# Hybrid attention block: VectorE's read of query sums ahead of the tile rotation, GpSimd's power as a step behind it

## The reference

```python
h = rms_norm(x, norm_g)
z = h @ w_in
aq, ak, av, ag, mq, mk, mv, mi, mf, mo, mgate = jnp.split(z, split_points(), axis=-1)
q = rms_norm(aq.reshape(B, L, 16, 64), q_norm_g)
k = rms_norm(ak.reshape(B, L, 2, 64), k_norm_g)
q = apply_partial_rope(q, cos, sin)
k = apply_partial_rope(k, cos, sin)
ya = sliding_window_sink_attention(q, k, v, sink) * jax.nn.silu(ag)
...
x = x + jnp.concatenate([ya, ym], axis=-1) @ w_out
```

## Time and profile before

| | us |
|---|---|
| median of 3 runs | 3036.69 |
| lowest and highest of them | 3030.43, 3037.66 |
| profiled execution, its own time | 3035.71 |
| span in its profile | 3033.9 |

### The profile page before, as it was taken

The page is one execution under the profiler, slowest core; times in us unless marked ns, Lnnn a source line. Parts: engine busy times, 40 slices in busy tenths (PEclk is TensorE's granted clock), DMA queues, the critical chain, the costliest instruction groups (busy, mean ns, idle before and its releaser), DMA issues.

```text
span 3033.9 us, 44921 instructions
## 1 busy us (share of the span) xinstructions
PE 2940.7 (97%) x18366; PEld 2567.2 (85%) x18366; DVE 1630.7 (54%) x3259; ACT 1263.1 (42%) x2640; POOL 186.2 (6%) x207
## 2 busy tenths in 40 slices
PE   8899999999999999999999999999999999999998
PEld 7888888988889889888888888887888888878886
DVE  6777545366674553677433565235677433565234
ACT  5455423255554232466324433223466324433222
POOL 2100000020000000200000000000100000000000
PEclk9999999999999999999999999999999999999999
DMA  3111322211113222322232222323322232222232
GB/s 115 49 51 55 107 69 63 84 52 54 56 52 114 69 84 77 115 82 76 84 112 91 73 81 77 97 97 98 113 84 76 81 114 85 75 84 84 97 97 77
DMA packets 99735, 250.24 MB, mean 82 GB/s; under 512 B 8597, under 2 KB 44845, under 8 KB 99274
## 3 DMA queue, kind: packets, MB, share of 16 engines
q1 hardware_dynamic: 99530, 247.37, 25.6%
HBM read 239.60 MB, written 6.50 MB: 81 GB/s over the span
## 4 chain that ended last, share of the span: by engine, by line
PE 80%; DVE 11%; ACT 5%; issue 2%; DMA 1%; POOL 1%; DVEq 0%; POOLq 0%; SPq 0%; ACTq 0%
PE ps L92 77%; PE ps L95 3%; ACT Z L98 2%; DVE Z L101 2%; DVE Z L109 2%; DVE cl L101 1%; DVE ZR L101 1%; ACT ch L98 1%; DMA st<-in_stream_dram 1%; DVE Z L105 1%; DVE stat L122 1%; POOL stat L101 1%; DVE stat L109 1%; DVE Z L119 1%; ACT sq L98 0%
## 5 line engine op out<-in xcount | busy, mean ns | idle before, releaser
L101 DVE TENSOR_TENSOR cl<-st,ch 128x1024 fp32r<-128x1024 f32 (+1 forms) x436 | 501.2, 1158 | 644.0 <-ACT ch L98 643.5
L92 PE MATMUL ps<-hl,ch 128*128 128x264 f32 (+1 forms) x2816 | 834.2, 339 | 0.0
L92 PE MATMUL ps<-hh,ch 128*128 128x512 f32 (+1 forms) x2624 | 805.4, 347 | 25.7 <-ACT Z L98 11.0
L92 PE MATMUL ps<-hh,cl 128*128 128x512 f32 (+1 forms) x2624 | 794.2, 342 | 0.0
L98 ACT ACTIVATE ch<-st 128x1024 fp32r<-128x1024 f32 (+1 forms) x436 | 429.0, 990 | 512.4 <-PE ps L92 434.5
L92 PEld LDWEIGHTS ps<-hl,ch 128*128 128x128 f32 x2816 | 486.1, 190 | 59.3
L92 PEld LDWEIGHTS ps<-hh,ch 128*128 128x128 f32 x2624 | 454.5, 190 | 96.5 <-ACT Z L98 16.8
L92 PEld LDWEIGHTS ps<-hh,cl 128*128 128x128 f32 x2624 | 455.0, 190 | 59.0
L92 PE MATMUL ps<-ZR,ch 128*128 128x264 f32 (+2 forms) x1856 | 446.2, 337 | 5.5 <-DVE cl L101 5.1
L98 ACT ACTIVATE Z<-ps 64x128 f32<-64x128 f32 (+7 forms) x506 | 217.3, 437 | 426.8 <-PE ps L92 317.8
L92 PEld LDWEIGHTS ps<-ZR,ch 128*128 128x128 f32 x1856 | 305.2, 190 | 48.7 <-issue 12.8
(11 more groups left out here) (133 smaller groups left out, 3213.5 us busy)
## 6 DMA issues: line engine op xcount, KB each, us to landing
st<-in_stream_dram SPq DMA_DIRECT2D x372, 512.0 KB, 3.5
st<-in_stream_dram SPq DMA_DIRECT2D x64, 256.0 KB, 3.2
Z<-decay_rows SPq DMA_DIRECT2D x8, 904.0 KB, 6.5
Z<-bias_lines SPq DMA_DIRECT2D x16, 448.0 KB, 3.6
ya_spill<-Z SPq DMA_DIRECT2D x8, 512.0 KB, 4.6
Z<-ya_spill SPq DMA_DIRECT2D x2, 2048.0 KB, 7.5
Z<-in_x_dram SPq DMA_DIRECT2D x4, 512.0 KB, 5.3
Z<-in_mem_dram SPq DMA_DIRECT2D x2, 1024.0 KB, 5.9
```

The source lines that it names most:

```text
L92: return Ins(self, self.e and self.e.matmul(o, a, b, start=start, stop=stop, skip_group_check=True))
L101: return Ins(self, self.e and self.e.tensor_tensor(o, a, b, op))
```

## The change

`chain` sorts the tiles under way by their stage, so that stage 0 comes first, then stage 1, then stage 2. The power becomes a step of its own, `qpow`, which is put behind all stages of the call.

```diff
         def chain():
 
             todo, st["turn"] = st["turn"], []
+            todo.sort(key=lambda y: y[2])
             for t, n, x in todo:
                 if t == 8 and x == 0:
                     put("qkn", l)
...
                 if x < (1 if t == 8 else 2):
                     st["turn"].append((t, n, x + 1))
+            for t, n, x in todo:
+                if t < 8 and x == 0:
+                    put("qpow", l, t)
...
-            def qsum(l, t, n):
+            def qpow(l, t):
                 ap = RQ[:, :, 2 * t:2 * t + 2]
                 pool.wait_ge(("ms", l, t), ("ones",))
                 pool.tensor_tensor(ap, ap, P("mhalf").unsqueeze(2).to_broadcast([128, 5, 2]), ALU.pow).then_inc(
```

More of the change, by code:

```diff
@@ L2670, in final @@
                 rsqrt(so[:, 8:12], 1024, ("so2",))
-            do = dict(sqa=sqa, dqkev=dqkev, dex=dex, hsc=hsc, memprep=memprep, dnorm=dnorm, final=final, nrml=nrml, load=load, rope=rope, qsum=qsum, vz=vz, mvones=mvones, pn=pn, bar=pool.bar)
+            do = dict(sqa=sqa, dqkev=dqkev, dex=dex, hsc=hsc, memprep=memprep, dnorm=dnorm, final=final, nrml=nrml, load=load, rope=rope, qpow=qpow, vz=vz, mvones=mvones, pn=pn, bar=pool.bar)
             for kind, *a in steps:
```

## The result

| | before | changed |
|---|---|---|
| median, us | 3030.99 (5 runs) | 3047.07 (5 runs) |
| lowest and highest | 3027.84, 3037.66 | 3045.61, 3049.34 |
| profiled execution, its own time | 3035.71 | 3047.07 |
| span, mean granted clock | 3033.9, 0.988 | 3045.2, 0.984 |

The ratio is 1.0049, with a 95% interval from 1.0038 to 1.0059: slower by half a percent, about 16 us. The forecast of 3045 and its range (3034 to 3051) hold the time; the class that I gave the most to, within 0.3%, does not.

A forecast was written before the change was run, and what follows sets the result against it. TensorE, busy for 97% of the span, was taken as the bound. Six tile pairs +2.2, clock +7.5 and layer starts -0.9 gave +8.8 us on 3035.7: 3044.5, said as 3045 for the median; range 3034 to 3051.

The forecast's parts named there:

- the class that I gave the most to: Whole kernel: measured time within 0.3%, 9 us, of the kernel before; chance 0.55.
- First move: At six tile pairs, VectorE's sum read of t+1 precedes t's rotation, 1.36 us earlier; the block's softmax gains 1.0 us.
- Second move: At six tile pairs, t+1's rotation precedes t's split, costing 1.36 us; TensorE's scores start 0.36 us later, both moves together.
- The power blocks VectorE: Rival: GpSimd's power holds VectorE off for its whole length at six tile pairs, 3058 to 3066 us; chance 0.06.
- The clock: At six tile pairs, two 1.2 us TensorE gaps become one of 2.8; clock falls at five, 1.5 us each: +7.5 us.
- VectorE's head start: After each tile pair's split, VectorE is 1.2 us ahead with its rotation already done; claimed to be worth nothing.
- The clock behind short waits: TensorE's granted clock around the short gaps was said to stay at 1.00 in the kernel before.
- The starts: Tiles 0 and 1 of both layers: VectorE's maximum 0.66 us sooner in the first, 0.2 in the second; together -0.9 us.
- Same or slower: Whole kernel: +8.8 us on the profiled 3035.7, median 3045; chance within 9 us 0.55, slower by more 0.41.
- Faster: Rival: softmax gains at least the rotation's 1.36 us, so the split wait does not grow; 3032 to 3034 us, chance 0.12.

The follow-up runs named there:

- Experiment 1: Changed kernel, but the split of tile t stays ahead of the rotation of tile t+1, so only the sum read moves: 3033.22 us, ratio 1.0001 to the kernel before.
- filled kernel: Changed kernel with 20 useless matmuls ahead of TensorE's wait for the split, at tiles 0, 2, 4, 6 only: 3033.01 us, ratio 0.9999 to the kernel before.
- experiment 3: Changed kernel with 20 useless matmuls before TensorE's wait for the split: at every tile 3042.22 us; at tiles 0, 2, 4, 6 3033.01; at 2, 4, 6 3031.04.
- experiment 6: The changed kernel, unaltered, timed a second time beside the kernel before: 3044.40 us, ratio 1.0041.
- late power: Changed kernel with GpSimd's power one call later, behind the cosine product of its own tile: 3034.28 us, ratio 1.0003 to the kernel before.
- at pairs: Changed kernel with 20 useless matmuls ahead of TensorE's wait for the split, at tiles 2, 4, 6 only: 3031.04 us, ratio 0.9993 to the kernel before.

## Why the prediction was right, and where it was not

- **First move: right.** The sum read came at 137.94 (I said 138.02), the power took 2.35 us (2.3), the cosine product started at 140.50 (140.5), the tiny products ended at 141.96 (142.0). Experiment 1 gives the move's own worth as 1.0 us a place, which is the 1.0 us by which I had the softmax ahead.
- **Second move: right.** The scores started at 147.24 (147.3). Its price alone is 1.35 us (1.36), and that of both 0.35 us a place (0.36), the difference of the filled kernel from the kernel before.
- **The power blocks VectorE: fell.** The rotation sum ran at 138.75 within the power (138.18 to 140.53) in its usual 0.71 us. In the section "SBUF: two separate sides" of "SBUF — State Buffer", the Trainium skill has whichever of the two engines comes first lock the other out for its whole instruction, where VectorE's has two inputs in SBUF and GpSimd's reads SBUF, as here. These rows do not bear that out for the power, which only waits for the VectorE instruction in progress; for the 528-wide cosine product they do: 1.23 us for products that take 0.35, ending 0.14 us behind it.
- **The clock: right in kind, too small.** "Five places of six" at 1.5 us gave 7.5; all six fell, at 1.5 to 1.6 us each, so 9.2 (experiment 3). With the order, 11.3 us would be expected; the traces show 10.7 at the six places, against my 9.7. The shortfall lies behind the third place of a layer: from its scores to the layer's last long wait the changed kernel takes 1.05 us more (47.43 against 46.38). The fall costs 1.46 there, as the filled kernel shows (45.97), and the new order gives 0.4 back: the kernel before waits 0.34 us at 287.50 for VectorE's last rotation, and the changed kernel, which has made that rotation earlier, doesn't. I had said that VectorE's head start is worth nothing.
- **The clock behind short waits: wrong, and it did no harm.** I wrote that the clock stays at 1.00 around the short gaps. That holds for the twelve of 1.2 us at the pair places. In the same trace it fell behind the waits of 0.75 and 1.14 us in front of 123.01 (experiment 3), and behind one of 1.39 us at 90.66 (0.72 granted from 92 to 98 us). The sum did not use this, but with these rows in view 1.63 us would not have looked safe in experiment 1.
- **The starts: right in size at the first layer.** Measured from the same instruction (74.57 and 75.03), the maximum came 0.84 us sooner (I said 0.66), and TensorE gained 0.6 us. In the second layer TensorE's stretch is 1.7 us shorter (37.50 against 39.22) where I said 0.2, but the clock was low for 13.7 us in the kernel before and for 6.8 in the changed one, so the order's share can't be read there. The clock fell behind the new wait, as I said it might, and the slack took it.
- **Same or slower: the step that failed is the last one.** I added +8.8 us to one profiled execution that was itself one of the slower ones of the kernel before (3035.71, clock 0.988), and took the median of three runs, 3036.7, as its middle. Many more runs put it at 3031 to 3034. That the absolute time came out within 2 us is in part luck: my loss was too small by 7 us and my base too high by 6. The difference of the medians, 16 us in the section on the result and 10 in experiment 6, is over the 9 us that I had put as the border.
- **Faster: fell for the reason given.** The softmax gained 1.0 us and the rotation cost 1.36. The rival's condition, that the cosine product keeps out of the tiny products, is what the late power does, and even then the order is 0.1 us a place behind the kernel before (61.43 against 61.31), and the ratio is 1.0003.

Two things stay open. Why the clock held behind 2.1 us in one kernel and fell behind 1.63 us in another is not settled: TensorE's work in front of the wait differs between them, and no run varied that by itself. And whether it falls at one place can differ between executions of one kernel. Behind the two short waits of 0.75 and 1.15 us ahead of the first place it fell in 10 of 24 layers (the twelve profiles of the table that have these waits, two layers in each), in both of the kernel before and in none of the two kernels filled at t even and at pairs. These falls cost 1.5 us each (24.38 against 22.85 us to the first place, in two profiles of the changed kernel). Whether the filling keeps them away or it was chance, so few profiles can't tell.

## What to carry to other kernels

Price a reordering by the shape of TensorE's waits and not by their sum: two waits of 1.2 us, 7 us apart, cost nothing beyond themselves here, while one of 3.0 us cost 1.5 us or more on top at eleven of twelve places. Where a trace of the kernel before shows falls behind shorter waits, count on them. Where two instructions on a side engine can be swapped, put the one that TensorE waits for first at both of its places (the sum read ahead of the rotation, and the split ahead of the rotation), since here one half of the sort was a gain and the other a larger loss. And set a forecast on many runs of the kernel before, or on the mean clock of the profiled one, when the effect is half a percent.

## What the runs showed of the hardware

- The granted clock fell behind waits of 1.6 us (five places of six), 2.6 us (four of six) and 3.0 us (eleven of twelve), in one order behind waits for the sum read of 1.67 to 1.96 us (two of six), and once in six behind 2.1 us in another. It never fell behind the 1.2 us waits of the kernel before at the pair places, but in the same kernel behind 0.75 and 1.14 us standing 2.1 us apart, in both layers. A fall costs 1.5 to 1.6 us where TensorE bounds what follows, and the two longer ones 2.7 and 3.0 us.
- With matmuls that compute nothing of use in the wait, the clock held at all six pair places in each of four kernels. 20 of them (2.49 us) at the six places gave back 13.4 us in the medians of one group of runs (3044.40 to 3031.04); 9.2 us of it are seen at the places. They cost nothing where they ended before the wait did, and 2 us from place to place where there was no wait.
- A power of ten columns on GpSimd takes 1.95 us, more than a product of 528 columns (1.32 us). A VectorE instruction in progress delays it (to 2.35 us), while it does not delay VectorE's sine product or rotation sum (0.70 and 0.71 us within it); the wide product delays VectorE's smallest instructions by 0.7 to 0.9 us.
